# Gated DeltaNet on GpSimd: three of the five masked gate tiles of a head are issued behind diagonals

## The reference, cut to what matters

```python
gc = jnp.cumsum(to_chunks(g), axis=-1)
diff = gc[..., :, None] - gc[..., None, :]
decay = jnp.where(incl, jnp.exp(jnp.where(incl, diff, 0.0)), 0.0)
kk = jnp.einsum('nbhid,nbhjd->nbhij', kc, kc)
a_mat = jnp.where(strict, bc[..., :, None] * kk * decay, 0.0)
rhs = jnp.concatenate([vc * bc[..., None], kc * (bc * jnp.exp(gc))[..., None]], axis=-1)
sol = lax.linalg.triangular_solve(a_mat, rhs, left_side=True, lower=True, unit_diagonal=True)
qk = jnp.einsum('nbhid,nbhjd->nbhij', qc, kc) * decay
```

## Time and profile before

| what | us |
|---|---|
| median of three runs | 2616.72 |
| the three runs | 2614.05, 2616.72, 2618.86 |
| the profiled execution | 2618.86 |
| its span in the trace | 2617.1 |
| PE busy | 2504.8 |
| DVE busy | 1393.0 |
| POOL busy | 858.4 |
| ACT busy | 811.8 |

### The profile page before, as it was taken

How to read it: one execution, slowest core, us unless ns; L and a number is a source line. 1 busy time by engine, 2 the same in 40 slices (tenths; PEclk the granted TensorE clock), 3 DMA queues, 4 the chain that set the end, 5 groups by cost and what they waited for, 6 DMA issues and landing times. The chain is left out here.

```text
span 2617.1 us, 40299 instructions
## 1 busy us (share of the span) xinstructions
PE 2504.8 (96%) x16246; PEld 2088.3 (80%) x16246; DVE 1393.0 (53%) x2110; ACT 811.8 (31%) x1745; POOL 858.4 (33%) x580
## 2 busy tenths in 40 slices
PE   5999999999999999999999989999899999997999
PEld 4768887887888888888888877887688888886887
DVE  6783665213456565565656564256865555555342
ACT  4222554101264554635454463101211111112010
POOL 1443652332324132323324131335433333322121
PEclk9999999999899999999999999999999999998999
DMA  7231322222000010101001011224411111113442
GB/s 271 72 81 53 122 109 90 97 73 81 17 18 25 18 33 9 34 9 42 25 18 33 2 42 57 97 97 126 158 57 49 49 49 49 49 36 102 140 129 90
DMA packets 52646, 177.01 MB, mean 68 GB/s; under 512 B 5360, under 2 KB 14960, under 8 KB 51184
## 3 DMA queue, kind: packets, MB, share of 16 engines
q1 hardware_dynamic: 50160, 170.24, 20.0%
q10 hardware_dynamic: 2304, 4.20, 0.4%
HBM read 148.20 MB, written 20.97 MB: 65 GB/s over the span
## 5 line engine op out<-in xcount | busy, mean ns | idle before, releaser
L201 PE MATMUL late_ps<-h_hi,late_w_hi 128*128 128x512 f32 x784 | 306.4, 391 | 5.8 <-ACTq L127 3.2
L203 PE MATMUL late_ps<-h_hi,late_w_lo 128*128 128x512 f32 x784 | 306.1, 390 | 0.0
L202 PE MATMUL late_ps<-h_lo,late_w_hi 128*128 128x512 f32 x784 | 306.0, 390 | 0.0
L1403 PE MATMUL late_ps<-h_hi,dn_w_hi 128*128 128x512 f32 (+1 forms) x640 | 248.2, 388 | 5.6 <-issue 5.6
L1403 PE MATMUL late_ps<-h_lo,dn_w_hi 128*128 128x512 f32 (+1 forms) x640 | 252.2, 394 | 0.0
L1403 PE MATMUL late_ps<-h_hi,dn_w_lo 128*128 128x512 f32 (+1 forms) x640 | 249.9, 390 | 0.0
L184 POOL CAST late_w_hi<-late_w_raw 128x1024 fp32r<-128x1024 f32 x76 | 79.2, 1042 | 505.9 <-issue 376.2
L191 POOL TENSOR_TENSOR late_w_lo<-late_w_raw,late_w_hi 128x1024 fp32r<-128x1024 f32 x76 | 204.0, 2685 | 6.1
L2444 DVE SCALAR_TENSOR_TENSOR ffn_u<-ffn_pad,vectors,ffn_u 128x1024 f32<-128x1024 f32 x88 | 194.5, 2210 | 3.1
L201 PEld LDWEIGHTS late_ps<-h_hi,late_w_hi 128*128 128x128 f32 x784 | 147.7, 188 | 37.3 <-issue 6.7
L202 PEld LDWEIGHTS late_ps<-h_lo,late_w_hi 128*128 128x128 f32 x784 | 147.6, 188 | 30.8 <-issue 0.2
(11 more groups left out here) (360 smaller groups left out, 6027.3 us busy)
## 6 DMA issues: line engine op xcount, KB each, us to landing
late_w_raw<-in_w_up SPq DMA_DIRECT2D x44, 512.0 KB, 3.5
down_w_raw<-in_w_down SPq DMA_DIRECT2D x32, 704.0 KB, 4.3
late_w_ada<-in_w_ada SPq DMA_DIRECT2D x8, 2048.0 KB, 8.4
dn_w_raw<-in_w_dn SPq DMA_DIRECT2D x32, 512.0 KB, 3.9
w_ada<-in_w_ada SPq DMA_DIRECT2D x8, 1024.0 KB, 11.1
at_w_raw<-in_w_mg_at SPq DMA_DIRECT2D x16, 512.0 KB, 4.0
late_w_raw<-in_w_mg_dn SPq DMA_DIRECT2D x16, 512.0 KB, 3.7
late_w_raw<-in_w_out SPq DMA_DIRECT2D x16, 512.0 KB, 3.8
```

What stands on the lines that cost most here:

```text
L201: pe.matmul(out, self.hi[j][:, k, :], xh, start=(k == 0), stop=False)
L202: pe.matmul(out, self.hi[j][:, k, :], xl, start=False, stop=False)
L203: mm = pe.matmul(out, self.lo[j][:, k, :], xh, start=False, stop=(k == self.kt - 1))
L1403: mm = pe.matmul(bank[at_bank(s)][:, 0:n], wt[:, k, :], x[:, k, t0:t0 + n], start=(rest == 0), stop=(rest == GROUP_MM - 1))
```

## The change

`masked_g` for steps 0 and 1 stays in front of `units`. That for steps 2, 3 and 4 is issued behind the diagonals of steps 0, 1 and 2. No instruction is added or taken away, and nothing changes on the other engines.

```diff
-            for bt in range(4):
+            for bt in range(2):
                 masked_g(bt)
             units()
             for bt in range(BT):
                 bqd.wait(pool, h * 5 + bt + 1)
                 pool.sem_inc(turns, 1)
                 pool.affine_select(flat(bf, bt), flat(bf, bt), pattern=[[0, 4], [1, P]], compare_op=ALU.not_equal,
                                    fill=E_SCALE, base=0, channel_multiplier=-1).then_inc(bfd.sem, 1)
-                if bt == 0:
-                    masked_g(4)
+                if bt + 2 < BT:
+                    masked_g(bt + 2)
```

## The result

The kernel with the change takes 2733.2 us (median of four runs, 2729.6 to 2743.2). The ratio to the kernel before is 1.0449, with a 95% interval of 1.042 to 1.0479, so it is slower by about 115 us. The forecast was 2715 us in a range of 2688 to 2752. The profiled execution took 2735.8 us with a span of 2734.0, which is 116.9 us more than the span before.

What follows compares the result with a forecast made beforehand. PE, busy for 96% of the span, was taken to bound the kernel. 2618.9 us profiled + 83.3 of stops + 15.3 of low clock = 2717.5, with the median 2.1 lower: 2715 us, range 2688 to 2752.

Steps and rivals of the forecast that it cites:

- PE sets the pace and a wait has no cover: In a head's preparation PE, in a hand-written order, is busy 14.96 of 15.7 us; time it stands has nothing to fill it.
- The move of `units` costs nothing: On POOL `units` (4.58 us) runs earlier, covered by 10.21 us of idle time; first diagonal 0.77 us earlier, costed at nothing.
- The chain of 1.98 us and a stop at each of 24 places: From DVE's end over POOL's diagonal and mask to PE's decay, steps 2 to 4: 3.47 us a stop, 83.3 us.
- The clock: PE's clock falls to 1.2 GHz after some stops: 9 stretches of 1.7 us, 15.3 us in the sum.
- I take one such stretch a head: One 3.4 us stretch of PE at half speed a head, a second in head 7, up to 1.7 us each.
- PE's clock is low in most bursts: Sign that the prediction is wrong: PE's work between the stops runs mostly at the lower clock level.
- The clock falls in every burst: Rival: PE at the lower clock in most or all bursts between stops, 86 us, 2752 to 2786 us; chance 0.09.
- Part is taken back: Rival: PE's later waits in a head, 8.6, 4.0 and 3.2 us, might vanish; 2684 us as a median; chance 0.08.
- not slower: Rival: PE comes to the decay later than the mask, at most 8.6 us gained, 2608 us as a median; chance 0.03.
- The masks are slow in their new place: Rival: POOL's moved masks take the longest time, 2.287 us, not 1.040; 30 us more, 2745; inside the range, no own chance.

Runs made afterwards that it cites:

- the kernel with one stop a head among dense work: Kernel before, with only the mask of step 4 moved from behind the diagonal of step 0 to behind that of step 2: 2663.6 us, ratio 1.0187.

## Why the prediction was right, and where it was off

- *PE sets the pace and a wait has no cover.* Right: the added waits and the slower matmuls are the whole of the difference (116.8 of 116.9 us), and no other wait of a head's preparation shrank. All other waits together changed by 2.3 us.
- *The move of `units` costs nothing.* Right on the time, shown by moving it alone (1.0001). The sum missed that it now runs beside DVE's normalisation and makes that 1.75 us longer; it had the room.
- *The chain of 1.98 us and a stop at each of 24 places.* Right: 1.92 us and 24 waits. The stop was put at 3.47 us from decay to decay, 83.3 in all. From start to start it is 3.41 at the first stop of head 2, less than 3.47 by the 0.06 us that the chain was put too long. With the clock held up by added work, the change as a whole costs 82.3 us of span. The waits themselves sum to only 76.6, for two reasons: a wait counts from the end of the last transpose and not from its start, and it is shorter where PE reaches it late at the low clock, 3.05 against 3.25 us.
- *Every mask behind a diagonal is late.* The prediction did not say this, but a reader might take it from there. One place earlier in the queue the same order is nearly free (0.13%), with a margin of 0.2 us.
- *The clock.* This term was mis-sized: 15.3 us forecast, 42.8 measured. "I take one such stretch a head" failed, for 23 of the 24 bursts have one, and head 2 alone shows three places with 13.6 us at 0.50 together, one after every stop. The reason given for it, that dense work between the stops keeps the clock up, is refuted by the kernel with one stop a head among dense work, which lost some 2.4 us a stop. The sum with the measured clock would have been 2618.9 + 83.3 + 42.8 = 2745 in the profiled execution, for 2735.8 measured; 6.7 of the 9 us are the waits, 83.3 against 76.6. So the 2715 us are too low by 18 because the clock is 27.5 too small and the stops are a little too large.
- *Its own sign of being wrong.* The prediction says that it is wrong if "PE's clock is low in most bursts", and that came true, in 23 of 24. The chain was right and the step on the clock was not. That the time still lies in the range is in part luck: the range was to end where a low clock in most bursts begins, and it held because most of the bursts were slow for 3.4 us and not throughout.
- *The rivals.* "The clock falls in every burst" had the better account of the clock, and was given 0.09: it fell in 23 of 24, but was low for the whole burst in only 6, so the price was half of the 86 us. The rule of the Trainium skill ("TensorE: Matmul & The Clock Gate", the section on HAM oscillation) points the right way. That every burst starts at the low clock is borne out at 16 of the 24 stops; at 7 the clock fell after PE's return, in head 2 by 1.7 us, and at one it did not fall. "Part is taken back" and "not slower" did not come about; the three small waits are the same to a tenth. "The masks are slow in their new place" did not either, with a median of 1.038 us.

## What to carry to other kernels

In an in-order queue the question is not how much work is moved but behind which wait it now stands, and whether that wait depends on work that the engine needing the result does just before it needs it: if so, the loop that was overlapped becomes a chain, once for each step. A tile that is made two steps ahead in the data can still be too late by one place in the queue, so its lead is measured as the time at which it is ready against the time at which it is needed. And a stop of TensorE in dense work is priced with the clock that follows it: here another 56% on the waits of three stops a head (42.8 on 76.6 us), and 74% on those of one (19.3 on 26.0), both to within the few us that the clock term can be read.

## What the runs showed of the hardware

- One stop of 3.25 us in otherwise dense matmul work brought the clock to the 1.2 GHz level for part of the work behind it at 6 of 8 places (19.3 us lost). Stops of 2.8 to 3.3 us, three in a row, did at 23 of 24 (42.8 us lost), stops of 1.9 us at 6 of 24 (25.9 us lost, a part of it elsewhere in the heads), and stops of 0.5 us at none (3.9 us, no more than the kernel before varies by itself). The shorter stops were made by filling the long ones with matmuls, so the work ahead of them differs too.
- Matmuls without use kept the clock up and paid for themselves: 66 us of them saved 32 us, because they stood where PE waited.
- Two 16-bit copies on GpSimd and one 32-bit product of DVE with both inputs in SBUF slowed each other: 2.98 us for 1.22 for the product, and 3.32 for 2.32 for the second copy. The first, which had begun before the product, kept its 2.32. The Trainium skill ("GPSIMD Engine Reference", the table with the SBUF interfaces) states such contention, and these rows agree; the size is theirs.
